# Last token tile's experts from gathered rows on VectorE instead of dense products on TensorE

## The reference, cut to what matters

```python
s = einsum('blhpd,hpnd->blhpn', q, sub_keys)           # 2 x 128 key scores per head
s_top, i_top = top_k(s, 16)
best, flat = top_k(s_top[..., 0, :, None] + s_top[..., 1, None, :], 16)
expert = i1 * 128 + i2                                  # 8 heads x 16 picks per token
gate = softmax(best)
act = gelu(einsum('ld,lkd->lk', xb, u_tab[e]))          # per head
y += einsum('lk,lkd->ld', act * gate, v_tab[e])
h = layer_norm(2 ** 0.25 * h + y)
```

## Time and profile before

| what | us |
|---|---|
| median of three runs | 3055.18 |
| the profiled execution | 3057.01 |
| its span, first to last instruction | 3055.2 |
| TensorE (PE) busy | 2809.9 |
| VectorE (DVE) busy | 1508.3 |
| ScalarE (ACT) busy | 931.8 |
| GpSimd (POOL) busy | 984.7 |

### The profile page before, as it was taken

One profiled execution on the slowest core, in us unless ns is written; L12 is line 12 of the kernel. 1 busy time (PEld: TensorE's weight loads), 2 busy tenths in 40 slices (PEclk: granted clock), 3 DMA queues, 4 the chain that ended last, 5 costly groups with the idle time before them and its releaser, 6 DMA issues. The chain is left out here.

```text
span 3055.2 us, 45413 instructions
## 1 busy us (share of the span) xinstructions
PE 2809.9 (92%) x15310; PEld 1500.3 (49%) x15310; DVE 1508.3 (49%) x3329; ACT 931.8 (30%) x1387; POOL 984.7 (32%) x488
## 2 busy tenths in 40 slices
PE   6999999959999999889899999999997999999996
PEld 3344344437776666744344444555543444444443
DVE  5213211147676666533248885444412565665664
ACT  4321221133333333222233333444432232333231
POOL 3320331222222222132334443333334444444443
PEclk9999999979999999999899999999998999999998
DMA  5211211110000000031414443868675666666662
GB/s 173 83 46 37 82 55 56 55 66 29 27 27 27 27 27 7 0 106 47 145 61 143 139 140 117 232 189 223 197 216 189 202 198 209 202 198 206 205 197 79
DMA packets 249547, 356.11 MB, mean 117 GB/s; under 512 B 145920, under 2 KB 146560, under 8 KB 249360
## 3 DMA queue, kind: packets, MB, share of 16 engines
q1 hardware_dynamic: 117392, 321.76, 31.9%
q10 hardware_dynamic: 132096, 33.56, 5.0%
HBM read 286.06 MB, written 69.21 MB: 116 GB/s over the span
## 5 line engine op out<-in xcount | busy, mean ns | idle before, releaser
L1750 POOL TENSOR_TENSOR hid_u_lo<-hid_u,hid_u_hi 128x1024 bf16<-128x1024 f32 x128 | 297.7, 2326 | 487.7 <-ACT hid_u_hi L1734 478.6
L146 PE MATMUL bank<-hT_hi,hid_u_hi 128*128 128x512 bf16 x1024 | 390.3, 381 | 22.6 <-POOL hid_u_lo L1750 21.5
L2200 PE MATMUL bank<-ex_v_hi,ex_gated_hi 128*128 128x512 bf16 x1024 | 389.2, 380 | 22.8 <-DVE ex_gated_lo L2255 22.8
L2234 POOL TENSOR_TENSOR ex_v_lo<-ex_v,ex_v_hi 128x1024 bf16<-128x1024 f32 x128 | 286.0, 2245 | 383.3 <-ACT ex_v_hi L2222 383.3
L146 PE MATMUL bank<-hT_lo,hid_u_hi 128*128 128x512 bf16 x1024 | 389.8, 381 | 0.0
L146 PE MATMUL bank<-hT_hi,hid_u_lo 128*128 128x512 bf16 x1024 | 389.6, 380 | 0.0
L2200 PE MATMUL bank<-ex_v_lo,ex_gated_hi 128*128 128x512 bf16 x1024 | 389.1, 380 | 0.0
L2200 PE MATMUL bank<-ex_v_hi,ex_gated_lo 128*128 128x512 bf16 x1024 | 389.1, 380 | 0.0
L201 POOL TENSOR_TENSOR ret_w_lo<-ret_w_raw,ret_w_hi 128x1024 bf16<-128x1024 f32 x72 | 152.9, 2156 | 402.5 <-ACT ret_w_hi L196 402.5
L2246 DVE TENSOR_TENSOR h<-h,bank 128x512 f32<-128x512 f32 x256 | 175.0, 684 | 179.0 <-PE bank L2200 177.6
L1742 ACT ACTIVATE hid_gelu<-bank 128x512 f32<-128x512 f32 x128 | 76.4, 597 | 389.1 <-PE bank L146 389.1
(11 more groups left out here) (409 smaller groups left out, 5355.7 us busy)
## 6 DMA issues: line engine op xcount, KB each, us to landing
hid_u<-in_peer_u SPq DMA_DIRECT2D x128, 512.0 KB, 3.7
ex_v<-in_peer_v SPq DMA_DIRECT2D x128, 512.0 KB, 4.6
expert_hidden<-hid_gelu SPq DMA_DIRECT2D x128, 256.0 KB, 2.2
expert_weights<-spread_grid ACTq DMA_DIRECT2D x64, 512.0 KB, 7.4
ex_gated<-expert_hidden SPq DMA_DIRECT2D x128, 256.0 KB, 2.7
ex_weights<-expert_weights SPq DMA_DIRECT2D x128, 256.0 KB, 2.9
ret_w_raw<-in_w_ret SPq DMA_DIRECT2D x60, 512.0 KB, 4.2
dn_w_raw<-in_w_dn SPq DMA_DIRECT2D x36, 512.0 KB, 3.4
```

Source lines behind the costliest of these rows:

```text
L146: last = nc.tensor.matmul(out, left[l], right[r], start=start and i == 0, stop=stop and i == len(PASSES) - 1)
L1750: self.nc.gpsimd.tensor_tensor(self.us[1][:, m % 2, :, :], self.u32[:, m % RING, :, :], self.us[0][:, m % 2, :, :], ALU.subtract).then_inc ...
L2200: last = nc.tensor.matmul(bank[:, :], gs[l][:, slot, t * P:(t + 1) * P], vs[r][:, slot, half * 512:(half + 1) * 512], start=j == 0 and i == 0,
L2234: nc.gpsimd.tensor_tensor(vs[1][:, m % 8, :], v32[:, m % RING, :], vs[0][:, m % 8, :], ALU.subtract).then_inc(s["v_lo"], 1)
```

## The change

The last token tile (tokens 384 to 511) leaves the dense path. DENSE is 384, and the moving operand of `form`, the GELU, the stored hidden values, the tables of `spread` and the units of `experts` shrink to it. Retrieval takes that tile first (`TILES`), and its picks are kept in token order as indices and weights (`note`). For each of its 128 picks, GpSimd gathers one row of u per token (128 rows of 4 KB, an indirect DMA) into a ring of four, which is the buffer of v that is idle then, and VectorE makes the dot product with the tokens by `tensor_tensor_reduce`: 16 beside each of the three later tiles, three per turn of spread (72), eight in the tail. ScalarE applies GELU to all 128 columns once. In `experts`, each step gathers one row of v per token and VectorE adds it, scaled, to the tokens' sum (`scalar_tensor_tensor`). Shares of Hidden's blocks in retrieval become 12, 20, 20, 20 (72 in all), spread has 48 and the tail 8. The six units of a group have a bank each.

```diff
+DENSE = SEQ - P
+TILES = (NT - 1,) + tuple(range(NT - 1))
+SHARES = (12, 20, 20, 20)
+PICKS = PH * TOPK
+BESIDE_TILE = 16
+BESIDE_TURN = 3
...
-            last = pair_matmul(self.nc, bank[:, :], view(self.us, slice(None), m % 2, kc),
-                               view(self.xs, slice(None), kc), kc == 0, kc == KC - 1)
+            last = pair_matmul(self.nc, bank[:, 0:DENSE], view(self.us, slice(None), m % 2, kc),
+                               view(self.xs, slice(None), kc, slice(0, DENSE)), kc == 0, kc == KC - 1)
...
+class Gathered:
...
+    def gather(self, pool, k):
+
+        pool.wait_ge(self.dotted, k + 1)
+        self.nc.gpsimd.indirect_dma_start(self.ring[:, k % RING, :], None, self.rows_dram[:, :],
+                                          bass.IndirectOffsetOnAxis(ap=self.index[:, k:k + 1], axis=0))\
+            .then_inc(self.arrived[k % RING], 16)
+
+    def dot(self, dve, k, slot, place):
+
+        dve.wait_ge(self.arrived[slot], (16 // RING) * (k - slot) + 16)
+        dve.wait_ge(self.dotted, k + (RING - 1))
+        self.nc.vector.tensor_tensor_reduce(self.spent[slot % 2], self.ring[:, slot, :], self.x, 1.0, 0.0,
+                                            ALU.mult, ALU.add, self.fresh[:, place:place + 1])\
+            .then_inc(self.dotted, 1)
...
-                over_blocks(pool, 0, blocks, lambda n, m: hidden.split_lo(pool, n, m))
+                for s in range(NT):
+                    for n in range(ends[s], ends[s + 1]):
+                        hidden.split_lo(pool, n, n)
+                        if s and n - ends[s] < BESIDE_TILE:
+                            gathered.gather(pool, (s - 1) * BESIDE_TILE + n - ends[s])
...
                         for i in range(n):
+                            if i == n // 2:
+                                beside()
                             ins = nc.vector.max(out[:, i, 0:8], values[:, i, :])
+                        beside()
                         step(ins)
...
-    busy = SEQ // G // per
+    busy = DENSE // G // per
+    dots_before = (NT - 1) * BESIDE_TILE
+    dots_beside = DENSE // (4 * G) * BESIDE_TURN
+    dots_last = PICKS - dots_before - dots_beside
...
                     hidden.store(sp, n, n)
+                    if n == BLOCKS - RING:
+                        sp.wait_ge(gathered.dotted, PICKS + RING)
                     incoming.load_values(sp, n - (BLOCKS - RING), n - (BLOCKS - RING))
...
+                            ins.then_inc(first_ready, 1)
+                            if u < BESIDE_TURN:
+                                j = q * BESIDE_TURN + u
+                                gathered.dot(dve, four * (RING * BESIDE_TURN) + (dots_before + j), j % RING, j)
...
-                over_blocks(pool, blocks, BLOCKS, lambda n, m: hidden.split_lo(pool, n, m))
+                k = dots_before
+                for n in range(blocks, BLOCKS):
+                    hidden.split_lo(pool, n, n)
+                    beside = n - blocks < busy
+                    for _ in range((1, 2)[n % 2] if beside else 2 if n < blocks + busy + dots_last // 2 else 0):
+                        gathered.gather(pool, k)
+                        k += 1
...
+            return range(UNITS * (m % GROUP) // GROUP, UNITS * (m % GROUP + 1) // GROUP)
...
-                        half, t = divmod(u, NT)
-                        bank = core.banks[4 + t]
-
-                        pe.wait_ge(s["added"], 2 * n + (u - 2 * GROUP - 2 * (m % GROUP) + 1))
+                    for u in units_of(m):
+                        half, t = divmod(u, TILES_IN)
+                        bank = core.banks[u]
+
+                        pe.wait_ge(s["added"], group * UNITS + (u + 1))
...
-                def step(n, m):
+                for n in range(BLOCKS):
+                    pool.wait_ge(s["row_added"], n + 1)
+                    nc.gpsimd.indirect_dma_start(row[:, n % RING, :], None, rows_dram[:, :],
+                                                 bass.IndirectOffsetOnAxis(ap=incoming.index[:, n:n + 1], axis=0))\
+                        .then_inc(row_in[n % RING], 16)
 
                     pool.wait_ge(s["v_hi"], n + 1)
...
                     if m >= GROUP:
-                        add_units(n, m)
+                        add_units(n, m, group)
+                    cols = slice(n, n + 1) if isinstance(n, int) else bass.ds(n, 1)
+                    dve.wait_ge(row_in[m % RING], arrived(n, m))
+                    dve.wait_ge(s["row_added"], n + RING)
+                    nc.vector.scalar_tensor_tensor(out=own, in0=row[:, m % RING, :],
+                                                   scalar=incoming.row_gated[:, cols], in1=own,
+                                                   op0=ALU.mult, op1=ALU.add).then_inc(s["row_added"], 1)
```

More of the change, by code:

```diff
@@ L1751, in split_lo, with __init__, note, keep @@
                                      self.us[0][:, m % 2, :, :], ALU.subtract).then_inc(self.u_lo, 1)
-def retrieve(core, weights, a, h1T, picked, hidden, blocks, ident):
+class Gathered:
+    def __init__(self, core, ctx, a, h0, incoming):
+        nc = self.nc = core.nc
+        self.rows_dram = a["peer_u_rows"]
+        self.x = h0[:, NT - 1, :]
+        self.ring = incoming.v
+        self.spent = [flat[:, :, :].rearrange("p a n -> p (a n)")[:, 0:D] for flat in (incoming.gated, incoming.weights)]
+        self.index_f = sbuf(nc, ctx, "row_index_f", [P, PICKS])
+        self.weight = sbuf(nc, ctx, "row_weight", [P, PICKS])
+        self.fresh = sbuf(nc, ctx, "row_fresh", [P, BESIDE_TILE])
+        self.dots = sbuf(nc, ctx, "row_dots", [P, PICKS])
+        self.index, self.gated = incoming.index, incoming.row_gated
+        self.arrived = [core.sem(f"row_in{i}") for i in range(RING)]
+        self.index_steps, self.dotted, self.kept, self.gelu, self.gated_done = (
+            core.sem("row_" + n) for n in ("index_steps", "dotted", "kept", "gelu", "gated"))
+    def note(self, dve, chosen):
+        nc = self.nc
+        flat = [chosen[:, j, :, :].rearrange("p h k -> p (h k)") for j in range(3)]
+        nc.vector.tensor_copy(self.weight[:, :], flat[0])
+        nc.vector.scalar_tensor_tensor(out=self.index_f[:, :], in0=flat[2], scalar=float(NK), in1=flat[1],
+                                       op0=ALU.mult, op1=ALU.add).then_inc(self.index_steps, 1)
+        dve.wait_ge(self.index_steps, 1)
+        nc.vector.tensor_copy(self.index[:, :], self.index_f[:, :]).then_inc(self.dotted, RING)
+    def gather(self, pool, k):
[9 more added lines that the diff above has]
+            .then_inc(self.dotted, 1)
+    def keep(self, dve, k, n, times):
+        cols = slice(k, k + n) if isinstance(k, int) else bass.ds(k, n)
+        dve.wait_ge(self.dotted, k + (n + RING))
+        self.nc.vector.tensor_scalar(self.dots[:, cols], self.fresh[:, 0:n], 1.0, None, ALU.mult)\
+            .then_inc(self.kept, 1)
+        dve.wait_ge(self.kept, times)
+    def apply_gelu(self, act, times):
+        act.wait_ge(self.kept, times)
+        self.nc.scalar.activation(self.dots[:, :], self.dots[:, :], ACT.Gelu).then_inc(self.gelu, 1)
+    def weigh(self, dve):
+        dve.wait_ge(self.gelu, 1)
+        self.nc.vector.tensor_tensor(self.gated[:, :], self.dots[:, :], self.weight[:, :], ALU.mult)\
+            .then_inc(self.gated_done, 1)
+        dve.wait_ge(self.gated_done, 1)
@@ L1761, in retrieve @@
+def retrieve(core, weights, a, h1T, picked, hidden, gathered, blocks, ident):
     nc = core.nc
     HP = 2 * PH
-    share = blocks // NT
+    ends = [sum(SHARES[:t]) for t in range(NT + 1)]
     LEAST = -3.0e38
@@ L1888, in _, with tile @@
                 dve.wait_ge(keys_in, 32)
-                with dve.Fori(0, NT) as t:
+                def tile(t, beside):
                     link = Chain(dve, dve_steps, 0, t, 18)
@@ L1951, in _, with beside, spread @@
                     link.ends_turn()
-def spread(core, a, picked, weights_dram, hidden, blocks, incoming):
+                tile(0, lambda: None)
+                gathered.note(dve, chosen)
+                with dve.Fori(0, NT - 1) as later:
+                    order = iter(range(BESIDE_TILE))
+                    def beside():
+                        j = next(order)
+                        gathered.dot(dve, later * BESIDE_TILE + j, j % RING, j)
+                    tile(later + 1, beside)
+                    gathered.keep(dve, later * BESIDE_TILE, BESIDE_TILE, later + 1)
+def spread(core, a, picked, weights_dram, hidden, gathered, blocks, incoming):
     nc = core.nc
@@ L1980, in spread @@
         TURN = SLOTS * G
-        bk = Banks(core, [(f"w{u}", u) for u in range(SLOTS)], SEQ // TURN)
-        spans = SEQ // SPAN
+        bk = Banks(core, [(f"w{u}", u) for u in range(SLOTS)], DENSE // TURN)
+        spans = DENSE // SPAN
         span_turns = SPAN // TURN
@@ L2043, in _ @@
+                for j in range(dots_last):
+                    k = PICKS - dots_last + j
+                    gathered.dot(dve, k, k % RING, j)
```

(13 more changed lines are left out.)

149 lines of the change are left out of this document (88 added, 61 removed).

## The result

The changed kernel is slower: 3151.15 us median of four runs (3143.83 to 3156.68) against 3055.78 for the kernel before in the same comparison, a ratio of 1.0311 with a 95% interval of 1.0286 to 1.0336. The profiled execution took 3149.25 us, its span 3147.4. The forecast was 3007 with a range up to 3095, so time and sign were both wrong.

The account below looks back on a forecast made before the run. TensorE was taken to bound every stage touched, with mutually exclusive GpSimd and two-SBUF-input VectorE work behind it. Terms +59 - 2 - 67 - 49 + 4 + 7 = -48 on 3057.0 gave 3009, less 1.8: 3007 us, range 2875 to 3095.

Parts of the forecast that it names:

- the spread block at 7.0: Spread stage, 48 blocks instead of 64: ports 6.5 and transfers 6.65 nearly coincide, 7.0 us taken, 336 us, -67.
- The upper end of 8.2: Spread block, slow end in us: transfers delayed, dots waiting, and what stands behind them in VectorE's order late for TensorE.
- Retrieval: Retrieval stage: one tile of 62.2 and three of 89.8, less 1.5, 330 us against 271.0: +59.
- the later tiles: Retrieval: 62.2 plus 27.6 for 16 dots and their waits for GpSimd's subtractions makes 89.8 us each.
- The gather's issue: GpSimd's time to issue one gather: no row, taken as 1.0 us between ends 0.33 and 2.13.
- the issue rival: GpSimd's queue becomes the bound: slower, sign decided from issues of about 2.6 us, 3101 at 3; chance 0.14.
- The step of 5.3: Experts' stage: row pass stands behind GpSimd's subtraction, so a step takes 5.3 us; stage 673 us, +7.
- The lower end of 4.45: Experts' step, fast end: transfers of 1.44 MB at 324 GB/s take 4.45 us.
- Preparation, tail and hand-over: Three smaller stages: preparation -2, tail 37 us against 85.7 (-49), hand-over +4 for four row additions.
- The ring of four starves the dots: Gathers wait for a free slot and GpSimd's next subtraction, then land late: spread block 8.2, tile 95, 3081; chance 0.12.
- The phases fall well: Engines interleave almost without loss: experts' step 4.5, transfer-bound, tiles may lose 9.4 us waits; 2880 to 2908; chance 0.22.
- My own sign for "wrong": Forecast is wrong if an experts' step is under 4.7 or over 5.7 us, or a spread block under 6.4.

## Why the prediction was wrong, and where it was right

**The step that failed** is the spread block at 7.0 (336 us, -67), and in it the sentence that compared resources: 6.5 for the ports, 6.65 for transfers, "GpSimd: 2.5 + 1.5 x 1.0 = 4.0". Each was a sum of work for one resource, and each came near: 6.41 without gathers, 6.87 down to 6.66 with the gathers placed early, and GpSimd busy for 187.7/48 = 3.9. The upper end of 8.2, for dots that wait, was an allowance without a working. What was not costed is the way round from engine to engine, although the text had all its links: "each gather stands on GpSimd between two subtractions", "behind it wait the spread's operands". Strung together, with a landing that the earlier trace rows put at 4.6 us for a plain load and that measured 5.8 for a gather, they make a loop that takes 17.9 us for two blocks. The stage came out 431.5 - 336 = 95 us over its forecast; the gathers issued earlier took 100 us off it.

**Retrieval** (+59 forecast, +87 measured) had its mechanism right and two terms too small. Tile 0 came at 63.3 for 62.2. For the later tiles, 98.8 for 89.8: a dot takes 2.10 us where 1.14 + 0.6 was put, and 3.8 us of waiting for rows per tile had no term; 16 x 0.36 + 3.8 = 9.6, against 9.0 missing. Why a dot waits for more than the average of a random meeting is not shown. GpSimd was busier than forecast, for 73.4 of a tile's 98.8 us, since most of the gathers' issues took 1.76 us there; and several dots run in a row. The run with tokens in PSUM shows the dot's own price: 1.21, for the assumed 1.14.

**The gather's issue** (1.0, bounds 0.33 and 2.13) was well sized when alone, 0.95 to 1.10, and reached 1.76 beside a row pass or a dot. In the token tiles that is the 1.7 from which the issue rival let GpSimd's queue pass 89.8 us, but GpSimd still stood for a quarter of each tile. The 2.6 that it needed to decide the sign was not reached; it is out.

**Experts.** The step of 5.3 and the reason for it held: 5.35, with row passes of 2.5 to 3.6 us behind subtractions, and the two ways around the meeting at that pass (order with early rows, or PSUM) both gave 4.6. The stage ran to +15 for +7. TensorE is busy for 555.5/680.9 = 82%, not near 73%: 2304 matmuls at 0.2168 us are 499.5 us, which at the granted clock of 0.90 become 555. The lower end of 4.45, by transfers, was not reached: about 4.6 is what four different kernels came to. Preparation, tail and hand-over were right within 7 us.

**The rivals.** "The ring of four starves the dots" (0.12; slower; 3081) came nearest. It gave the right sign and named the cause in half a sentence, "after GpSimd's next subtraction", but blamed the number of slots and stopped at 8.2 us. The same four slots with earlier gathers give 6.87. It should have had the larger chance, since nothing in the rows spoke against it. "The phases fall well" (2880 to 2908) failed as drawn: early gathers alone end at 3046. All the edits together reached 2924, still above it. My own sign for "wrong", a spread block under 6.4 or a step out of bounds, had no upper mark for the block, the side on which it failed.

Not tried: the gathers of the token tiles placed earlier, though rows are still late there (31.6 us over three tiles in the run with tokens in PSUM); other shares of dots between tiles and spread stage; and how much of the remaining 6.7 us of a block is ScalarE's issue of the weight stores, which took 5.1 us in the block shown and stands ahead of the split. That part stays open.

## What to carry to other kernels

Where one engine's ordered queue mixes work that others wait for with transfers that are wanted later, follow one item the whole way round before summing anything: if the way back to its own issue holds a landing, the loop's length and not the busiest resource sets the pace, and moving the issue ahead by a few items within the same slots, here three in a ring of four, can take it out. When two limits lie close together, an edit that lifts one alone may show nothing, as two did here; test the pair before giving either up.

## What the runs showed of the hardware

**A gather's issue is held by VectorE too.** Where VectorE has no operation with two SBUF inputs under way, it takes about 0.95 us. In the changed kernel's experts' stage it takes 1.76 when it begins during the held row pass, and it ends 0.83 after the pass (2710.57 + 1.76 against 2711.51); with the pass reading its sum from PSUM the mean is 1.10. A plain addition of two SBUF inputs holds it too: in the run with tokens in PSUM a gather issued at 1663.68, during the 2.28 us addition of 2048 elements of 1663.60, takes 3.03. The Trainium skill (SBUF — State Buffer, "SBUF: two separate sides") describes the ports that VectorE and GpSimd share as an exclusive lock that whoever starts first keeps. For the subtraction of 2708.30 the rows agree: the pass begun at 2708.98 ends 1.09 us after it, as if it had begun then. The pass of 2702.70 was held although its record begins before that of the subtraction, so recorded starts do not always tell which engine was first. The page limits the lock for operations with two SBUF inputs to GpSimd operations that read SBUF. The gather takes its row numbers from an SBUF tile and may count among them; no run separates that from the rest of its issue.

**TensorE's clock** is lower where TensorE waits more. TensorE's timeline in the spread stage of the changed kernel:

```profile
1990.64 0.33 PE L146 MATMUL bank<-hT_lo,hid_u_hi 128*128 128x384 bf16 x1
1990.80 0.33 PE L146 MATMUL bank<-hT_hi,hid_u_lo 128*128 128x384 bf16 x1
1993.58 0.28 PE L2171 MATMUL bank<-spread_second,spread_first_hi 128*128 128x128 bf16 x1 [2.45 <-DVE spread_first_lo L2145]
...
2003.12 0.53 PE L146 MATMUL bank<-hT_hi,hid_u_lo 128*128 128x384 bf16 x1
2003.44 0.38 PE L146 MATMUL bank<-hT_hi,hid_u_hi 128*128 128x384 bf16 x1
2003.65 0.33 PE L146 MATMUL bank<-hT_lo,hid_u_hi 128*128 128x384 bf16 x1
2003.82 0.33 PE L146 MATMUL bank<-hT_hi,hid_u_lo 128*128 128x384 bf16 x1
```

Before the wait of 2.45 us matmuls of 384 columns start 0.16 us apart, the 2.4 GHz level; after it and a second wait of 3.21 us they start 0.32 apart, the 1.2 GHz level (2003.12 to 2003.44), and from 2003.65 0.17 again. The mean clock of this stage is 0.81, 0.91 once the gathers come early and 0.95 without them: it rises as the waits shrink.

**Transfers** of 512 KB and 192 KB, from the queues of SP and GpSimd together, run at 311 to 315 GB/s with the engines 0.90 to 0.92 busy in the experts' stage. That is a little under the 324 that the forecast took from the earlier trace rows.
